# Neighbourhood attention: queries and keys as upper and lower parts, scores as three products

## The reference, cut to what matters

```python
qkv  = (h  @ na_w_qkv[j] + na_b_qkv[j]).reshape(B, T, 3, N_HEADS, HEAD_DIM_2)
qkvc = (hc @ na_w_qkv[j] + na_b_qkv[j]).reshape(B, K, 3, N_HEADS, HEAD_DIM_2)
...
s_lat = jnp.einsum('bnqhd,bjnmhd->bhnqjm', q_row, k_blk)      # q_row is q * Dh ** -0.5
s_lat = jnp.where(valid_j, s_lat + bias, MASK_VALUE)
s_ctx = jnp.einsum('bnqhd,bkhd->bhnqk', q_row, kc)
p = jax.nn.softmax(jnp.concatenate([s_lat, s_ctx], axis=-1), axis=-1)
o = p_lat @ v_blk + p_ctx @ vc
y = o @ na_w_o[j] + na_b_o[j]
```

## Time and profile before

| | |
|---|---|
| median of 3 runs | 2614.68 us (2612.6 to 2616.1) |
| the profiled execution's own time | 2617.16 us |
| its span in the profile | 2615.1 us |
| TensorE matmuls (PE), busy | 2499.9 us, 96% |
| VectorE (DVE), busy | 1745.0 us, 67% |
| ScalarE (ACT), busy | 1092.4 us, 42% |
| mean granted TensorE clock, share of full speed | 0.986 |
| neighbourhood stage, first query projection to last transpose of O | about 2174 to 2383 us of the span |
| attention rounds in it | 2251 to 2380 us |

### The profile page before, as it was taken

One profiled execution on the slowest core, in us unless ns is written; L12 is line 12 of the kernel. 1 busy time (PEld: TensorE's weight loads), 2 busy tenths in 40 slices (PEclk: granted clock), 3 DMA queues, 4 the chain that ended last, 5 costly groups with the idle time before them and its releaser, 6 DMA issues.

```text
span 2615.1 us, 35165 instructions
## 1 busy us (share of the span) xinstructions
PE 2499.9 (96%) x13498; PEld 2089.6 (80%) x13498; DVE 1745.0 (67%) x2562; ACT 1092.4 (42%) x1876; POOL 366.2 (14%) x414
## 2 busy tenths in 40 slices
PE   4999999999999999999989999999999999999998
PEld 3678987779979878877648887888888888777997
DVE  6967986858995776776865565675565665345454
ACT  3466544556554212236644322224322224334543
POOL 1101101001111100104831110100100100000101
PEclk9999999989999999999989999999999999999999
DMA  7645885536783554542102343453352443321462
GB/s 302 217 174 176 292 304 198 189 133 210 242 275 113 185 185 151 183 165 73 65 17 81 113 174 116 161 176 107 113 185 105 175 163 113 97 73 65 162 196 94
DMA packets 118293, 413.01 MB, mean 158 GB/s; under 512 B 13552, under 2 KB 17776, under 8 KB 118128
## 3 DMA queue, kind: packets, MB, share of 16 engines
q1 hardware_dynamic: 117568, 409.06, 44.9%
q10 hardware_dynamic: 560, 1.72, 0.2%
HBM read 409.68 MB, written 1.05 MB: 157 GB/s over the span
## 4 chain that ended last, share of the span: by engine, by line
PE 62%; DVE 4%; ACT 2%; issue 1%; POOL 1%; DVEq 0%; POOLq 0%; ACTq 0%
PE ps L1102 18%; PE ps L1104 18%; PE ps L1103 18%; PE ps L1318 2%; PE ps L1295 1%; PE ps L1255 1%; PE ps L1286 1%; DVE sl L1673 1%; DVE F L1790 1%; PE ps L1266 1%; DVE mjunk L1687 1%; POOL ap L2184 1%; ACT F L1440 1%; DVE ps L2027 0%; PE ps L1341 0%
## 5 line engine op out<-in xcount | busy, mean ns | idle before, releaser
L1102 PE MATMUL ps<-hH,sh 128*128 128x256 f32 (+1 forms) x2560 | 842.4, 329 | 6.9 <-DVE hL L1761 3.5
L1103 PE MATMUL ps<-hL,sh 128*128 128x256 f32 (+1 forms) x2560 | 835.7, 326 | 0.0
L1104 PE MATMUL ps<-hH,sl 128*128 128x256 f32 (+1 forms) x2560 | 835.6, 326 | 0.0
L1673 DVE TENSOR_TENSOR sl<-raw,sh 128x1024 fp32r<-128x1024 f32 x534 | 649.5, 1241 | 92.2 <-ACT sh L1381 91.6
L1381 ACT ACTIVATE sh<-raw 128x1024 fp32r<-128x1024 f32 x534 | 540.4, 1039 | 391.4 <-PE ps L1104 323.9
L1687 DVE CUSTOM_DVE_ANT_0 mjunk<-raw,cB,V 128x1024 bf16<-128x1024 f32 x384 | 539.1, 1404 | 29.9 <-DMA C<-in_cst 8.3
L1102 PEld LDWEIGHTS ps<-hH,sh 128*128 128x128 f32 x2560 | 482.3, 188 | 59.6 <-issue 8.5
L1104 PEld LDWEIGHTS ps<-hH,sl 128*128 128x128 f32 x2560 | 481.4, 188 | 48.2
L1103 PEld LDWEIGHTS ps<-hL,sh 128*128 128x128 f32 x2560 | 480.9, 188 | 48.7 <-issue 1.7
L2157 POOL TENSOR_TENSOR uLl<-F,uHh 128x256 fp32r<-128x256 f32 (+1 forms) x132 | 166.3, 1260 | 1203.0 <-ACT uHh L1562 1103.4
L1102 PE MATMUL ps<-sh,uHh 128*128 128x512 f32 x792 | 314.7, 397 | 10.5 <-DVE sl L1673 10.3
(11 more groups left out here) (168 smaller groups left out, 2250.5 us busy)
## 6 DMA issues: line engine op xcount, KB each, us to landing
raw<-in_w SPq DMA_DIRECT2D x756, 512.0 KB, 4.5
raw<-in_w SPq DMA_DIRECT2D x16, 256.0 KB, 3.8
cB<-in_rpb SPq DMA_DIRECT2D x64, 64.0 KB, 2.6
X<-in_x ACTq DMA_DIRECT2D x1, 1024.0 KB, 11.8
X<-in_ctx SPq DMA_DIRECT2D x1, 1024.0 KB, 7.4
out<-X SPq DMA_DIRECT2D x2, 512.0 KB, 2.7
raw<-in_w SPq DMA_DIRECT2D x2, 288.0 KB, 5.7
cB<-in_c ACTq DMA_DIRECT2D x1, 512.0 KB, 5.5
```

The costliest lines, as they stand in the source:

```text
L1102: self.e.matmul(out, lh, rh, start=start, stop=False)
L1103: self.e.matmul(out, lh, rl, start=False, stop=False)
L1104: return self.e.matmul(out, ll, rh, start=False, stop=stop)
L1673: self.e.tensor_tensor(lo[:, 0:w], raw[:, 0:w], hi[:, 0:w].bitcast(F32), ALU.subtract).then_inc(self.sems["w_lo"], 1)
```

## The change

The queries are kept as `qH` and `qL` (float32r, 8 pairs each), the keys as `kH` and `kL` in a ring of two blocks each, for pair c in block c % 2, instead of `qT` and `kT` (float32). DVE writes the biased projection to one of the three `F` buffers (float32), ACT rounds it to the upper part (`qk2` of `Scalar`), DVE subtracts (`qk2_lo`). The scores of an item are `mm3`: three float32r products with 64 channels. The `qk2_lo` step is put off: it is added after the next projection, or in front of the next round.

```diff
@@ -373,6 +373,7 @@
                 it["S"] = self.place("S", k % 3)
                 if st["what"] == "na":
                     it["BM"] = self.place("BM", k % 8)
+                    it["kT"] = st["keys"][it["h"] // 2]
                 self.add("att_s", st=st, it=it, i=k)
                 if st["what"] == "mix":
                     self.left(it["sc"])
@@ -759,11 +760,22 @@
         gid = self.gates_later("mod_w_2", l, 5, 1.0, 1, True)
         nid = self.new()
 
+        late, keys = [], []
+
+        def lowers():
+            while late:
+                late.pop(0)()
+
         def part(p, c):
             N = 256 if p == 0 else 512
             b = self.product(name, (0,), p * 1024 + c * 128, slice(0, N), ("h", hid))
-            self.add("qk2", part=p, c=c, b=b, nid=nid, u=self.u_at)
+            lowers()
+            g = dict(part=p, c=c, b=b, nid=nid, u=self.u_at, f=self.next("F", 3), k=self.place("kH", c % 2) if p else None)
+            if p:
+                keys.append(g["k"])
+            self.add("qk2", **g)
             self.left(b)
+            late.append(lambda: self.add("qk2_lo", **g))
 
         def vdone(t, half, b):
             self.add("v2", t=t, half=half, b=b, nid=nid, u=self.u_at)
@@ -776,7 +788,7 @@
         items = [dict(kind=h // 8, i=i, h=h, heads=[h], den=i * 16 + 8 * (h // 8), first=h % 8 == 0,
                       last=h % 8 == 7, n=512, nh=1, row=(i, h // 8))
                  for h in range(16) for i in range(2)]
-        rounds = self.attend(dict(what="na", mid=nid, out=out), items)
+        rounds = self.attend(dict(what="na", mid=nid, out=out, keys=keys), items)
         loads = [lambda it=it, k=k: self.add("bias_load", it=it, slot=k % 8, use=k // 8, nid=nid)
                  for k, it in enumerate(items)]
 
@@ -1009,6 +1022,12 @@
     def buf(self, place):
         return self.m[place[0]][place[1]]
 
+    def qk_parts(self, s):
+
+        if s["part"]:
+            return [self.m[n][s["k"][1]][:, :] for n in ("kH", "kL")]
+        return [self.m[n][:, s["c"], :] for n in ("qH", "qL")]
+
     def col(self, src):
 
         if src[0] == "gc":
@@ -1235,7 +1254,7 @@
         self.done("mm", ("full", s["b"]))
 
     def att_s(self, s):
-        it, st = s["it"], s["st"]
+        it, st, left = s["it"], s["st"], []
         ps = self.buf(it["sc"])
         self.wait_ge(self.gone(it["sc"]))
         i = slice(it["i"] * 128, (it["i"] + 1) * 128)
@@ -1252,9 +1271,12 @@
             pr = slice(64 * j, 64 * j + 64)
             self.wait_ge(self.got("qk2", st["mid"], 0, c))
             self.wait_ge(self.got("qk2", st["mid"], 1, c))
-            x = self.e.matmul(ps[:, :], self.m["qT"][pr, c, i], self.m["kT"][pr, c, :], start=True, stop=True)
+            kh, kl = self.m["kH"][it["kT"][1]], self.m["kL"][it["kT"][1]]
+            x = self.mm3(ps[:, :], self.m["qH"][pr, c, i], self.m["qL"][pr, c, i], kh[pr, :], kl[pr, :], True, True)
+            if j and it["i"]:
+                left = [("left", it["kT"])]
         x.then_inc(self.sems["mm"], 1)
-        self.done("mm", ("full", it["sc"]))
+        self.done("mm", ("full", it["sc"]), *left)
 
     def att_t(self, s):
         it = s["it"]
@@ -1353,7 +1375,7 @@
                           pout=self.pout, qturn=self.qturn, idx=self.idx, att_e=self.att_e, att_c=self.att_c,
                           glu1_a=self.glu1_a, glu1_b=self.glu1_b, glu1_c=self.glu1_c,
                           glu2_a=self.glu2_a, glu2_b=self.glu2_b, cglu_a=self.cglu_a, tap_w=self.tap_w, tap_p=self.tap_p,
-                          ln_sq=self.ln_sq, ln_rstd=self.ln_rstd, ln_out=self.ln_out, v2=self.v2,
+                          ln_sq=self.ln_sq, ln_rstd=self.ln_rstd, ln_out=self.ln_out, qk2=self.qk2, v2=self.v2,
                           u_free=self.u_free)
 
     def start(self, s):
@@ -1635,6 +1657,17 @@
         self.e.activation(self.m["hH"][:, c, :], F, ACT.Copy).then_inc(self.sems["a_sb"], 1)
         self.done("a_sb", ("hc_hi", s["hid"], c), *([("ln_act", s["cid"])] if c == KD - 1 else []))
 
+    def qk2(self, s):
+        part, c = s["part"], s["c"]
+        self.wait_ge(self.got("qk_f", s["nid"], part, c))
+        if s["k"]:
+            self.wait_ge(self.gone(s["k"]))
+        if s["u"]:
+            self.wait_ge(self.got("u_free", s["u"]))
+        self.e.activation(self.qk_parts(s)[0], self.buf(s["f"])[:, 0:512 if part else 256], ACT.Copy).then_inc(
+            self.sems["a_sb"], 1)
+        self.done("a_sb", ("qk_hi", s["nid"], part, c))
+
     def v2(self, s):
         t, half = s["t"], s["half"]
         if t % 2 == 0:
@@ -1657,7 +1690,8 @@
                           gated=self.gated, pout=self.pout, qturn=self.qturn, idx=self.idx, rank=self.rank,
                           att_s=self.att_s, att_c=self.att_c, att_n=self.att_n, oscale=self.oscale, glu1_a=self.glu1_a,
                           glu1_b=self.glu1_b, glu2_a=self.glu2_a, cglu_v=self.cglu_v, tap_v=self.tap_v, ln_sq=self.ln_sq, ln_rstd=self.ln_rstd,
-                          ln_out=self.ln_out, qk2=self.qk2, v2=self.v2, final=self.final_scale)
+                          ln_out=self.ln_out, qk2=self.qk2, qk2_lo=self.qk2_lo, v2=self.v2,
+                          final=self.final_scale)
 
     def start(self, s):
         self.e.wait_ge(self.sems["ld0"], 16)
@@ -2067,16 +2101,25 @@
 
     def qk2(self, s):
         part, c, b = s["part"], s["c"], self.buf(s["b"])
+        N = 512 if part else 256
         bias = self.vec("na_b_qkv_2", (0,), part * 8 + c)
+        F = self.buf(s["f"])[:, 0:N]
         self.wait_ge(self.got("full", s["b"]))
-        if s["u"]:
-            self.wait_ge(self.got("u_free", s["u"]))
+        self.wait_ge(self.gone(s["f"]))
         if part == 0:
-            x = self.e.tensor_scalar(self.m["qT"][:, c, :], b[:, 0:256], bias, 0.125, ALU.add, ALU.mult)
+            x = self.e.tensor_scalar(F, b[:, 0:256], bias, 0.125, ALU.add, ALU.mult)
         else:
-            x = self.e.tensor_scalar(self.m["kT"][:, c, :], b[:, :], bias, None, ALU.add)
+            x = self.e.tensor_scalar(F, b[:, :], bias, None, ALU.add)
         x.then_inc(self.sems["v_ps"], 1)
-        self.done("v_ps", ("left", s["b"]), ("qk2", s["nid"], part, c))
+        self.done("v_ps", ("left", s["b"]), ("qk_f", s["nid"], part, c))
+
+    def qk2_lo(self, s):
+        part, c = s["part"], s["c"]
+        F = self.buf(s["f"])[:, 0:512 if part else 256]
+        hi, lo = self.qk_parts(s)
+        self.wait_ge(self.got("qk_hi", s["nid"], part, c))
+        self.e.tensor_tensor(lo, F, hi.bitcast(F32), ALU.subtract).then_inc(self.sems["v_sb"], 1)
+        self.done("v_sb", ("left", s["f"]), ("qk2", s["nid"], part, c))
 
     def v2(self, s):
         t, half = s["t"], s["half"]
@@ -2219,14 +2262,15 @@
             + [(f"wd{i}", [P, 13, P], F32) for i in range(2)] + [(f"ap{i}", [P, 512], F32) for i in range(2)]
             + [(f"FT{i}", [P, 512], F32) for i in range(4)],
             [("uHh", [P, KF * 256], F32R), ("uLl", [P, KF * 256], F32R)],
-            [("qT", [P, KD, 256], F32), ("kT", [P, KD, 512], F32), ("v", [P, 4, D], F32), ("O2", [P, 2, D], F32)],
+            [("qH", [P, KD, 256], F32R), ("qL", [P, KD, 256], F32R), ("kH0", [P, 512], F32R), ("kH1", [P, 512], F32R),
+             ("kL0", [P, 512], F32R), ("kL1", [P, 512], F32R), ("v", [P, 4, D], F32), ("O2", [P, 2, D], F32)],
             [("qkT", [P, 21, 256], F32), ("v1", [P, 2, D], F32), ("O1", [P, 2, D], F32),
              ("stg0", [P, 2, 512], F32), ("stg1", [P, 2, 512], F32), ("stk", [P, 2, 72], F32), ("ki20", [P, 128], F32), ("ki21", [P, 128], F32), ("sc0", [P, 128], F32),
              ("sc1", [P, 256], F32)],
         ]))
         m["UP"] = [m[f"UP{i}"] for i in range(3)]
         m["FT"] = [m[f"FT{i}"] for i in range(4)]
-        for n in ("wd", "ap"):
+        for n in ("wd", "ap", "kH", "kL"):
             m[n] = [m[n + "0"], m[n + "1"]]
 
         m["stg"] = [m["stg0"], m["stg1"]]
```

## The result

| | before | changed kernel |
|---|---|---|
| median of 20 runs each, side by side | 2614.57 us (2610.87 to 2617.25) | 2619.53 us (2615.74 to 2626.06) |
| ratio | | 1.0019, 95% interval 1.0013 to 1.0025 |
| profiled execution: own time / span | 2617.16 / 2615.1 us | 2623.8 / 2622.0 us |
| mean granted TensorE clock | 0.986 | 0.984 |
| start of the value projection's last group of three products to start of the first product of the output projection | 140.88 us | 145.88 us |

What follows compares the result with a forecast made beforehand. PE was taken as the bound, with work in 96% of the span and two early waits. +1.28 + 1.85 - 4.6 + 3.4 = +1.9 us gave a median of 2616.6 us against 2614.68, range 2610.5 to 2621.5.

Steps and rivals of the forecast that it cites:

- Scores: Each score on PE falls from 1.06 to 0.89 us, gaining 0.17; items 5 to 31 gain 4.6 us.
- three records for each score, 0.23 apart: Sign of being right in the profile after: each score's three products start 0.23 us apart, 0.89 to the next transpose.
- the low bound: Score gain at least 0: three products at 0.32 plus 0.20 give 1.16, but overlapping loads argue against that loss.
- The changes of type and of rows: Extra 0.09 or 0.12 us around scores: stays if from 64 rows; rival, type change, gains 0.29 per score, chance 0.11.
- First gap: PE's wait before the first scores grows from 0.94 to 2.39 us through rounding and subtraction; net loss 1.28.
- Second gap: Before item 0's transposes at key block 1, rounding and table load delay the exponentials: gap about 3.05 us, loss 1.85.
- L: Start of the last product of a key block's projection, from which the prediction counted; 2257.95 for key block 1.
- Other key blocks: No loss at later key blocks: exponentials behind the rounding are ready with 0.48 and 0.38 us to spare.
- the rival of the ACT queue: Rounding holds back exponentials at six later key blocks; 1 us beyond the threshold means +6, 2622.6 us; chance 0.15.
- The query blocks: First six query blocks cost nothing: six roundings and six subtractions, under 0.7 us each, before the value projection.
- Clock: Half-speed falls behind both gaps, each 3.4 us long and costing 1.7: +3.4 together; rival without falls or with one, chance 0.13.
- The 1.76 and 1.39 of the earlier trace: PE gaps before the change: 1.76 us was followed by a fall to half speed, 1.39 was not.

Runs made afterwards that it cites:

- one-product experiment: Kernel with late roundings and query block 5 moved, but each score one float32 product of the upper parts instead of three float32r; 2614.07 us, ratio 0.9997.
- both: Changed kernel with roundings and subtractions queued behind later rounds and query block 5's projection moved behind key block 0's; 2607.31 us, ratio 0.9966 against the kernel before.

## Why the prediction was right, and where it was off

- **Scores: right in the sum, not in its parts.** Predicted 0.89 to the next transposes, measured 0.88 to 0.89; on items 5 to 31, -4.43 for -4.6. The one-product experiment gives 0.17 by the rows and 0.16 over 31 scores. But the sum was 3 x 0.23 + 0.20, with all the change-over at the end, and the sign was "three records for each score, 0.23 apart". The steps are 0.33, 0.24 and 0.31: the first product takes 0.10 more than 0.23 and the last 0.08 more. That they make up the same 0.2 is luck; the first 0.10 was named only for the low bound.
- **The changes of type and of rows, right.** The product ahead of a score still takes 0.33 (2300.80 - 2300.47; 0.32 before) and the step from the last PV product group to a score 0.93 (2303.11 - 2302.18; 0.93 before). Neither extra went, so neither was the price of the change of type. By the Trainium skill (TensorEngine Tiling (Array Packing), Key Properties) a change of tiling mode drains the engine, and the rows fit it: the change to 64 rows stayed, and so did the extras.
- **First gap, right.** 2.32 for 2.39, and +1.23 for +1.28.
- **Second gap, right.** The transposes of item 0 came at L + 4.35 (2268.77 - 2264.42) for 4.32, the gap was 3.06 for 3.05. The order on ACT was as worked out, and the exponential starts 0.02 after the table load ends (2267.58 - 2266.28 - 1.28). The drain of about 1.38 us which the Trainium skill adds (ScalarE: Activation LUTs, What ACT_TABLE_LOAD costs) is not in this trace.
- **Other key blocks, right.** No wait stands on PE between the second gap and the last item's end, where the 1.32 ahead of PV products was there before the change as well. The spare of some 0.4 us was enough; the rival of the ACT queue is out.
- **The query blocks, right.** From the first query product to the first value product it took 20.1 us in both.
- **Clock: that it falls, right; one size, wrong.** The step that failed is "so I count both: +3.4", and in it the length of the fall, taken for both gaps from the one row. The first was that (3.4 us, +1.53). The second lasted 10.2 us and cost 18.25 - 12.15 - 1.85 = 4.25 in place of 1.7; filling that gap alone gave 4.23 back. This is +2.55 of the 3.07 by which the stretch exceeds the sum. I had also put the bound for each at "about 3.4", so the true value lay outside my bounds for that term. That the time still lies in the range is luck: the range reached up to 2621.5 for the sake of other mechanisms, which did not come, and not for a longer fall.
- **The last item**, from the transposes of item 30 on, +0.57, is most of the rest, and its cause is not shown: the clock falls there for 6.8 us in both kernels. Counted from the last score, the end lies between 15.38 and 16.64 us over the ten kernels, in code that is the same in all of them but for the last score itself. The clock tells the two groups apart: where it falls there for 3.4 us the end takes 15.38 to 15.48 (three kernels), where it falls for 6.8 us 16.01 to 16.64 (the other seven, the kernel before among them). The changed kernel, and the one with query block 5 moved:

```profile
2382.00:2396.00 14.00, 11.41 (x62) 10.18 (x61) 9.29 (x20) 6.11 (x14) 0.00 (x0) 0.76 0.03 8
2376.00:2390.00 14.00, 11.27 (x61) 9.77 (x62) 9.18 (x19) 6.54 (x14) 0.00 (x0) 0.88 0.11 35
```

**The kernel before had shown both kinds of fall.** The prediction read one row of its trace. The same trace has longer falls elsewhere. Here are a wait ahead of transposes in the attention of the first block, a wait ahead of a dense projection, and the windows behind them:

```profile
539.61 0.44 PE L1266 MATMUL ps<-C,S 128*128 128x128 f32 x2 [1.74 <-ACT S L1522]
1365.49 0.47 PE L1102 MATMUL ps<-sh,hH 128*128 128x512 f32 x1 [3.72 <-DVE hL L2064]
```

```profile
538.00:558.00 20.00, 16.38 (x63) 12.84 (x64) 8.55 (x16) 11.13 (x35) 0.00 (x0) 0.66 0.35 127
1364.00:1372.00 8.00, 6.51 (x22) 5.23 (x23) 4.19 (x7) 5.05 (x8) 2.57 (x2) 0.79 0.00 0
```

That is 0.34 x 20 / 0.5 = 13.6 us at the lower clock behind a wait of 1.74, and 0.21 x 8 / 0.5 = 3.4 us behind one of 3.72. Behind waits of 1.76, 2.52 and 2.53 ahead of dense projections (785, 966 and 1154 us) the fall is 3.4 us as well. Behind waits of 1.73 and 1.66 ahead of transposes of attention (165 and 499 us) it is 10.2 and 6.8, at 499 us with a second wait of 1.20 and a projection right behind. Two much longer waits, of 4.11 and 5.97 ahead of other products (1238 and 1346 us), have 6.8 and 10.2. The second gap of the changed kernel is one ahead of transposes of attention, so the trace of the kernel before gave 6.8 to 13.6 us for its fall, and not 3.4.

What stays open is the cause of the length. Known is: waits of 1.76 to 3.72 with 128-row projections behind them (five places; at the first gap a single score stands between) give 3.4 us; the second gap, at 3.06 (two traces) and at 1.64 (one), followed by rounds of attention (64-row scores, transposes, short PV products), gives 10.2 us each time. That the work behind the gap sets the length fits all of these, but in the first block further waits of 0.75 to 1.89 follow the first one, the two longest waits don't belong to either kind, and no kernel put attention work behind the first gap or a projection behind the second. Nor does the code alone fix the length, since the end, where the code is the same, shows 3.4 us in the executions of some kernels and 6.8 in those of others. What sets off a fall is open too. The 1.76 and 1.39 of the earlier trace rows are no boundary: behind a wait of 1.99 at 416 us in the kernel before the clock stays at 1.00 up to 424 us, where a fall of 3.4 us begins, and behind one of 1.85 at 421 us in the changed kernel it stays there up to 430 us. At the end of the changed kernel waits of 1.32 and 1.06 are enough for a fall.

## What to carry to other kernels

A step that shortens PE's work by moving work to other engines has to be priced where PE has no other work queued: the first round of a pipeline, not its steady state. The saving here (0.17 us on each of 32 scores) was real, and was eaten by two waits, which grew from 1.6 to 5.4 us together, and above all by the lower clock behind them, 5.8 us. For the price of a new wait on PE look through the whole trace of the kernel before for waits with the same kind of work behind them, and take the longest fall as the bound. Before paying for it, look for an independent projection that can stand in the gap, and on the queue of the busy helper engine put new steps behind those that PE waits for: the two moves together turned +0.19% into -0.34%.

## What was unexpected of the hardware

- Two clock falls within 20 us lasted 3.4 and 10.2 us, and the long one kept its length when its gap was cut from 3.06 to 1.64 us. Waits of 0.84 and 0.85 ahead of item 1's transposes brought no fall. At the end of the stage, in the same code, the fall was 3.4 us in the executions of three kernels and 6.8 in those of seven.
- Unread products in the gap are enough to keep the clock: five and six of them (ten and twelve records, 2.32 and 2.86 us) saved 5.56 us, although neither the first score nor item 0's transposes started earlier behind the projection ahead of them.
- Two scores whose operands lie in different halves of the rows still run side by side when each is three products. In "both", two such scores take 0.90 together (2258.61 to the transposes at 2259.51), no longer than one (start, length, record; x2 is a pair of records that overlap):

```profile
2258.61 0.50 PE L1127 MATMUL ps<-kH,qH 64*128 64x512 f32 x2
...
2259.51 0.66 PE L1294 MATMUL ps<-C,S 128*128 128x128 f32 x4
```
